# An S5 stage with its table copies moved ahead of the output writes, and merge and feed-forward blocks reordered by one tile

## What is computed

```python
_, _, s_re, s_im = lax.associative_scan(combine, (a_re, a_im, bu_re, bu_im), axis=1)
y = einsum('blgp,ghp->blgh', s_re, c_re) - einsum('blgp,ghp->blgh', s_im, c_im) + u * d_skip
y = gelu(y);  v = y @ w_glu + b_glu;  y = v[..., :D_S5] * sigmoid(v[..., D_S5:])
```

```python
x = x + g1 * ((sigmoid(pc) * y_conv + sigmoid(pa) * y_attn) @ w_out[l])
u = dwconv1d(h2 @ w_up[l], dw, dw_b);  a, g = split(u, 2)      # 3 taps, 22 tiles each
x = x + g2 * ((silu(g) * a) @ w_down[l])
```

## Time and profile before

| | |
|---|---|
| three runs | 3112.88, 3113.59, 3116.96 us (median 3113.59) |
| profiled execution | 3104.09 us, its span 3102.3 us |
| mean granted clock of TensorE | 0.968 of full speed |
| busy | PE 2876.4 us (93%), PE loads 75%, DVE 1513.3 us (49%), POOL 1266.3 us (41%), ACT 1084.9 us (35%) |
| chain that ended last | PE 77%, DVE 9%, issue 5%, DVE queue 3%, ACT 3%, DMA 1% |
| S5 stage | from about 362 us to 517.7 us of the span |
| merges of the latent passes | 1570 to 1606 us and 2611 to 2647 us |
| feed-forward blocks | 1672 to 2240 us and 2705 to 3085 us |

### The profile page before, as it was taken

One profiled execution on the slowest core, in us unless ns is written; L12 is line 12 of the kernel. 1 busy time (PEld: TensorE's weight loads), 2 busy tenths in 40 slices (PEclk: granted clock), 3 DMA queues, 4 the chain that ended last, 5 costly groups with the idle time before them and its releaser, 6 DMA issues.

```text
span 3102.3 us, 42343 instructions
## 1 busy us (share of the span) xinstructions
PE 2876.4 (93%) x15864; PEld 2340.5 (75%) x15864; DVE 1513.3 (49%) x2050; ACT 1084.9 (35%) x1593; POOL 1266.3 (41%) x696
## 2 busy tenths in 40 slices
PE   6999878999999998999889999999889998799997
PEld 6975635877777887777768888888777777687786
DVE  6865574451224453387745423313247876532324
ACT  4445122332233232236324412313243453252332
POOL 3452101443544370687523322222348773344342
PEclk9989988999999999999989999999999999899998
DMA  5227495322332333422212212212223222233231
GB/s 177 92 82 263 149 273 186 108 94 83 109 92 84 110 116 128 124 79 72 68 55 69 75 55 68 61 55 63 73 89 96 72 65 71 72 93 91 88 96 67
DMA packets 115574, 306.88 MB, mean 99 GB/s; under 512 B 36128, under 2 KB 44448, under 8 KB 114784
## 3 DMA queue, kind: packets, MB, share of 16 engines
q1 hardware_dynamic: 86000, 284.22, 29.1%
q10 hardware_dynamic: 28864, 18.76, 2.1%
q0 software_dynamic: 560, 1.84, 0.2%
HBM read 294.95 MB, written 7.45 MB: 97 GB/s over the span
## 4 chain that ended last, share of the span: by engine, by line
PE 77%; DVE 9%; issue 5%; DVEq 3%; ACT 3%; DMA 1%; ACTq 1%; POOL 0%; SPq 0%; POOLq 0%
PE ps L295 37%; PE ps L325 18%; PE ps L316 6%; PE ps L1860 3%; DVE co L2153 2%; PE ps L2266 2%; DVEq L2154 2%; PE ps L1918 2%; PE ps L1864 1%; PE ps L1865 1%; PE ps L1868 1%; DMA wraw<-stream 1%; DVE mv L2344 1%; PE ps L1937 1%; PE ps L701 1%
## 5 line engine op out<-in xcount | busy, mean ns | idle before, releaser
L256 POOL TENSOR_TENSOR wlo<-wraw,whi 128x1024 fp32r<-128x1024 f32 x373 | 923.1, 2484 | 1503.0 <-ACT whi L248 1501.6
L248 ACT ACTIVATE whi<-wraw 128x1024 fp32r<-128x1024 f32 x373 | 392.3, 1055 | 760.0 <-PE ps L316 300.8
L295 PE MATMUL ps<-xhi,whi 128*128 128x512 f32 (+1 forms) x1328 | 469.9, 370 | 1.9 <-issue 1.7
L295 PE MATMUL ps<-xlo,whi 128*128 128x512 f32 (+1 forms) x1328 | 470.6, 371 | 0.0
L295 PE MATMUL ps<-xhi,wlo 128*128 128x512 f32 (+1 forms) x1328 | 334.0, 371 | 0.0
L295 PEld LDWEIGHTS ps<-xhi,whi 128*128 128x128 f32 x1328 | 240.5, 188 | 48.7 <-issue 2.7
L295 PEld LDWEIGHTS ps<-xlo,whi 128*128 128x128 f32 x1328 | 240.5, 188 | 44.4
L295 PEld LDWEIGHTS ps<-xhi,wlo 128*128 128x128 f32 x1328 | 232.3, 188 | 44.7
L2153 DVE SCALAR_TENSOR_TENSOR co<-ub,vec,co 128x512 f32<-128x512 f32 (+1 forms) x216 | 230.1, 1105 | 5.4 <-issue 0.5
L1062 DVE SCALAR_TENSOR_TENSOR res<-ps,mod,res 128x512 f32 (+1 forms) x64 | 47.6, 748 | 266.6 <-PE ps L316 155.1
L2252 POOL TENSOR_TENSOR co<-co,ct 128x512 f32<-128x512 f32 (+1 forms) x144 | 165.2, 1147 | 20.8 <-issue 0.4
(11 more groups left out here) (396 smaller groups left out, 5614.6 us busy)
## 6 DMA issues: line engine op xcount, KB each, us to landing
wraw<-stream SPq DMA_DIRECT2D x425, 512.0 KB, 3.5
wada<-w_ada SPq DMA_DIRECT2D x56, 512.0 KB, 6.4
wraw<-w_ada SPq DMA_DIRECT2D x40, 512.0 KB, 4.0
biasb<-attn_bias ACTq DMA_DIRECT2D x32, 256.0 KB, 3.8
xin<-x0T SPq DMA_DIRECT2D x4, 528.0 KB, 6.7
s_u<-uk ACTq DMA_DIRECT2D x8, 264.0 KB, 3.3
res<-x0T ACTq DMA_DIRECT2D x1, 2048.0 KB, 8.9
s_y<-yk ACTq DMA_DIRECT2D x64, 32.0 KB, 4.1
```

Of the source, the lines that this page charges most:

```text
L248: act.activation(whi[:, s], wraw[:, s], ACT.Copy).then_inc(hi_done[s], 1)
L256: pool.tensor_tensor(wlo[:, s], wraw[:, s], whi[:, s].bitcast(F32), ALU.subtract).then_inc(lo_done[s], 1)
L295: last = pe.matmul(ps[:, bank, 0:b - a], w[:, s, kt], x[:, kt, c0 + a:c0 + b], start=start, stop=stop)
```

## The change

In the S5 stage `s5_head_act` is divided. `s5_bat_act` (the copy of `bat`) now stands between GELU and the DMAs of y; `s5_kernel_act` (`ka`, `dec`) stays behind them. Tile 0's turned tables go to PSUM banks 4 to 7, and PE does `s5_bat_pe(0)` and `s5_k_pe(0)` ahead of the last of the four single output units, `s5_w_pe(0)` right after it. DVE does `s5_diagonal(0)` and `s5_tables(1)` ahead of its last add of that projection. `ada_used` becomes one semaphore in place of eight. In the merge DVE forms `mlo` of tile m-1 after `mv` of tile m. In the feed-forward `split_hi` comes after the middle tap, and the product, the rounding and the rest of tile m-1 come after the taps of tile m (the last tile's directly behind). The `Fori` loops of both are written out. In `kv_act` the tiles rounded after the four units are (0,1), (2,3), (4), (5,6,7) in place of two each.

```diff
     def ada_worked(eng, u):
-        eng.wait_ge((lo_done if u < ADA_RAW else ada_used)[s], rnd + 1)
+        if u < ADA_RAW:
+            eng.wait_ge(lo_done[s], rnd + 1)
+        else:
+            eng.wait_ge(ada_used, u - ADA_RAW + 1)
     def s5_dve(dve):
-        s5_diagonal(dve, 0)
-        s5_tables(dve, 1)
         for i in range(NT):
     def s5_pe(pe):
         pe.wait_ge(s_m0, 1)
+        s5_w_pe(pe, 0)
+        g = U_GLU - 2
+        pe.wait_ge(acc_free[g % R], read_out(g))
+        ada_pe(pe, ADA_SSD, ADA_SSD + ADA_HEAD)
         all_freed(pe, U_GLU)
-        s5_bat_pe(pe, 0)
-        s5_k_pe(pe, 0)
-        ada_pe(pe, ADA_SSD, ADA_SSD + ADA_HEAD)
-        s5_w_pe(pe, 0)
         s5_bat_pe(pe, 1)
         s5_k_pe(pe, 1)
+    def head_bank(i):
+        return 0 if i else 4
...
             act.activation(yk[:, i % 2]..., ps[:, 6:8, ...], ACT.Gelu).then_inc(f_g.sem, 1)
+            if i + 2 < NT:
+                s5_bat_act(act, i + 2)
             act.wait_ge(f_g.sem, f_g.past("g", i))
             ...
             for k in range(LB):
                 act.dma_start(yd[i % 2]..., yk[16 * k:16 * k + 16, i % 2]).then_inc(s_yw[i % 2], 16)
             if i + 2 < NT:
-                s5_head_act(act, i + 2)
+                s5_kernel_act(act, i + 2)
...
     def raw_pe(pe, U, n, xh, xl, sums, late=None):
         for j in range(R):
+            if late and j == R - 1:
+                late()                      # s5_bat_pe(pe, 0); s5_k_pe(pe, 0)
             pe_unit(pe, U + R + j, 0, 0, xh, xl, SEQ)
...
     def kv_act(act, p, then):
-            for kt in (2 * j, 2 * j + 1):
+            for kt in ((0, 1), (2, 3), (4,), (5, 6, 7))[j]:
...
     def merge_dve(dve, p, then=None):
+        def lo(m):
+            dve.wait_ge(p.m_h.sem, p.m_h.past("hi", m))
+            dve.tensor_tensor(mlo[:, m, 0:T], mv[:, m % 2, 0:T], mhi[:, m, 0:T]..., ALU.subtract)
+        for m in range(NT):
             ... gc, ga as before ...
+            dve.tensor_tensor(mv[:, m % 2, 0:T], gc, ga, ALU.add).then_inc(p.m_v.sem, 1)
+            if m:
+                lo(m - 1)
...
     def ffn_act(act, p, q):
                     act.wait_ge(unit_done[s], rnd + 2)
-                    split_hi(act, U + 2 * j + k + R, i, 1)
                     act.wait_ge(p.f_v.sem, p.f_v.past("h", t, 2))
                     ins = act.activation(f[:, j, k, 0:T], ps[:, s, 0:T], ACT.Identity, ...)
+                    split_hi(act, g + R)
                 ... Silu of tile m ...
+                if m:
+                    hi(m - 1)
+            hi(n - 1)
...
     def ffn_dve(dve, p, q):
                 ... both units' taps of tile m ...
+                if m:
+                    gate(m - 1)             # wait silu and hi; product, rest
+            gate(n - 1)
...
             s5_tables(dve, 0)
-            for m in range(R, NT):
+            for m in range(R, NT - 1):
                 add_unit_dve(dve, U_OUT1 + m, 0, 0, m, res, SEQ, r=r)
+            dve.drain()
+            s5_diagonal(dve, 0)
+            s5_tables(dve, 1)
+            add_unit_dve(dve, U_OUT1 + NT - 1, 0, 0, NT - 1, res, SEQ, r=r)
```

More of the change, by code:

```diff
@@ L189, in build @@
     ada_landed = [sem(f"ada_landed{s}") for s in range(RA)]
-    ada_used = [sem(f"ada_used{s}") for s in range(RA)]
+    ada_used = sem("ada_used")
     s_in = [sem(f"inputs_landed{h}") for h in range(4)]
@@ L2327, in merge_dve @@
         all_freed(dve, p.U + 36)
[L2329 to L2343, removed]
-                dve.tensor_tensor(v, gc, ga, ALU.add).then_inc(p.m_v.sem, 1)
-                dve.wait_ge(p.m_h.sem, p.m_h.past("hi", m))
-                dve.tensor_tensor(mlo[:, m, 0:T], v, mhi[:, m, 0:T].bitcast(F32), ALU.subtract).then_inc(p.m_v.sem, 1)
-        if p.one:
-            body(0)
-            body(1)
-        else:
-            loop(dve, 2, body)
+        def lo(m):
+            dve.wait_ge(p.m_h.sem, p.m_h.past("hi", m))
+            dve.tensor_tensor(mlo[:, m, 0:T], mv[:, m % 2, 0:T], mhi[:, m, 0:T].bitcast(F32), ALU.subtract).then_inc(p.m_l.sem, 1)
+        for m in range(NT):
+            s, rnd = slot(p.U + 36 + m)
+            if p.one:
+                norm_add(dve, then.norm(0), m, then.T)
+            dve.wait_ge(unit_done[s], rnd + 2)
+            gc, ga = gt[:, m, 0:T], gt[:, m + NT, 0:T]
+            dve.tensor_tensor(gc, ps[:, s, 0:T], gc, ALU.mult)
+            dve.tensor_tensor(ga, ps[:, s + R, 0:T], ga, ALU.mult).then_inc(acc_free[s], 1)
+            dve.drain()
+            if p.one:
+                dve.tensor_tensor(m1[:, m, 0:T], gc, ga, ALU.add).then_inc(p.m_w.sem, 1)
+                continue
+            dve.tensor_tensor(mv[:, m % 2, 0:T], gc, ga, ALU.add).then_inc(p.m_v.sem, 1)
+            if m:
+                lo(m - 1)
+        if not p.one:
+            lo(NT - 1)
     def ffn_units(p):
@@ L2495, in ffn_dve, with gate @@
[L2495 removed]
+            def gate(m):
+                dve.wait_ge(p.f_s.sem, p.f_s.past("silu", t0 + m))
+                if m >= 2:
+                    dve.wait_ge(p.f_h.sem, p.f_h.past("hi", t0 + m - 2))
+                j = m % 2
+                dve.tensor_tensor(gated[:, j, 0:W], f[:, j, 1] if q else fs[:, j, 0, 0:T], f[:, j, 0, 0:W], ALU.mult).then_inc(p.f_v.sem, 1)
+                dve.wait_ge(p.f_h.sem, p.f_h.past("hi", t0 + m))
+                dve.tensor_tensor(hl[:, m, 0:W], gated[:, j, 0:W], h[:, m, 0:W].bitcast(F32), ALU.subtract).then_inc(p.f_v.sem, 1)
@@ new lines, in ffn_dve @@
+            for m in range(n):
+                t, j = t0 + m, m % 2
+                for k, name in enumerate("ag"):
+                    s = slot(U + 2 * m + k)[0]
+                    dve.wait_ge(p.f_a.sem, p.f_a.past(name, t))
+                    spans = [(s, 0, T)] + ([(R + s, T, W)] if q else [])
+                    for bank, a, b in spans:
+                        o = f[:, j, k, a:b]
+                        dve.scalar_tensor_tensor(o[:, 1:], ps[:, bank, 0:b - a - 1], col(f"fw0{l}", t + 22 * k), o[:, 1:], ALU.mult, ALU.add)
+                    dve.drain()
+                    for bank, a, b in spans:
+                        o = f[:, j, k, a:b]
+                        ins = dve.scalar_tensor_tensor(o[:, 0:b - a - 1], ps[:, bank, 1:b - a], col(f"fw2{l}", t + 22 * k), o[:, 0:b - a - 1], ALU.mult, ALU.add)
+                    ins.then_inc(acc_free[s], 1)
+                if m:
+                    gate(m - 1)
@@ L2654, in _ @@
             ssd_pe(pe)
-            raw_pe(pe, U_OUT1, "ssd", hhi, hlo, lambda: raw_sums_ssd(pe))
+            raw_pe(pe, U_OUT1, "ssd", hhi, hlo, lambda: raw_sums_ssd(pe), lambda: s5_first_pe(pe))
             s5_pe(pe)
```

97 lines of the change are left out of this document (43 added, 54 removed).

## The result

The changed kernel took 3090.02 us (median of 5 runs, 3080.33 to 3091.89), the kernel before 3113.59 (5 runs beside them, 3108.16 to 3117.56): ratio 0.9921, 95% interval 0.9903 to 0.9939, faster by 0.8% (the interval is 19 to 30 us). The forecast was 3101.9 with a range of 3089.0 to 3111.0: the sign and the range held, the gain was twice what I had worked out, 23.6 us for 11.7. The profiled execution went from 3104.09 to 3082.22 us, -21.9.

A forecast was written before the change was run, and what follows sets the result against it. PE, busy 93% of the span, was taken as the bound except in S5, ordered by ACT's list and y's round trip. +2.3 - 5.2 - 5.8 - 3.0 = -11.7 us gave 3092.4, plus 9.5 carried to medians: 3101.9, range 3089 to 3111.

The forecast's parts named there:

- S5: head: S5 start: turning tile 0's tables before PE's last output unit starts the chain 7.2 us earlier, less 1.4: -5.8 us.
- S5: copy ahead of the writes, tiles 0 to 4: S5 loop: y's writes wait for the `bat` copy; only 2.8 of the head's 5.8 us left, then +3.1 and +2.0.
- merges: Two merges: DVE omits its 0.79 us wait at both ends, POOL still sets 4.6 us a tile; 2.6 each, -5.2 us.
- feed-forward: Ends of six feed-forward blocks: tap ahead of `whi` shortens the chain by 0.97 us each, unrolling gives nothing; -5.8 us.
- context values: Context values: ACT's last `whi` follows an earlier rounding, on PE's path; -3.0 us.
- What is new is that y's writes wait for the copy: S5 loop on ACT: y's writes wait for the copy, the copy for PE, PE for DVE's tables two tiles ahead.
- Each such tile pays the 1.02 us of the copy: +3.1: S5 tiles 1, 2 and 3: y's round trip sets the pace, so the copy's time is added in each.
- tile 4's +2.0: S5 tile 4: writes wait 3.0 us for the turned tables, 2 counted since `ka` had to wait for PE too.
- fill the gap: Rival: earlier `wada` loads fill tile 4's idle DMA, S5 gives -12.6 instead of +2.3, 3087 us; chance 0.14.
- 6.8 us of idle DMA: S5 tile 4: idle DMA time, 15.5 x 0.44, which earlier loads could fill if DMA work sets the stage.
- slip ahead of POOL: Rival: in the merges DVE starts before POOL, giving 17.0 us instead of 5.2, 3090 us; chance 0.12.
- The burst: Rival: y's writes fall into the `wada` load burst; S5 pays +24 on top, 3126 us, slower; chance 0.07.

The follow-up runs named there:

- writes_wait: Changed kernel plus one ACT wait: the copy of `bat` must finish before y's writes are issued; 3094.5 us, ratio 0.993.
- split_first: Changed kernel with `split_hi` back ahead of the first tap in the feed-forward, the rest of the rewriting kept; 3096.24 us, ratio 0.994.
- small_loads: Changed kernel with 48 of the S5 loop's 56 `wada` loads cut to an eighth, part of the result omitted; 3075.47 us, ratio 0.989.
- lo_timed: Changed kernel, merge only: ACT splits one unit further ahead, POOL's subtraction timed to run beside DVE's gate products; 3074.82 us, ratio 0.987.
- late_and_timed: Changed kernel with the `bat` copy back behind y's writes, plus lo_timed's merge; 3074.7 us, ratio 0.988.

## Why the prediction was right in sign and short by half

| term | predicted | in the two traces | by experiment |
|---|---|---|---|
| S5: head | -5.8 | | -9.2 (164.4 to 155.3) |
| S5: copy ahead of the writes, tiles 0 to 4 | +3.0 + 3.1 + 2.0 | writes held 4.5 us longer | +3.6 (155.3 to 158.9) |
| S5 in all | +2.3 | -5.1 | -5.6 |
| merges | -5.2 | -2.63 and -2.65 | |
| feed-forward | -5.8 | 3 x 1.30 + 3 x 1.28 = -7.7 | 6 x 1.03 + 6 x 0.27 |
| context values | -3.0 | -3.0 | |
| sum | -11.7 | -21.1, and -0.8 between | |

The sign of the whole held by the last three terms, which came out near their sizes or above. S5 was forecast slower and became faster, and the missing gain is mostly there.

**The step that failed: "What is new is that y's writes wait for the copy", and with it "Each such tile pays the 1.02 us of the copy: +3.1" and tile 4's +2.0.** They are held only where the copy itself waits for PE: in tile 0 in every trace of the early order (1.8 us longer in the changed kernel, up to 2.9 in others, for my 3.0), and in tile 2 in two of the three traces with the changed kernel's S5 code (2.7 and 2.9 us). In the changed kernel tiles 1, 3, 4 and 5 issue their first write 0.6 us after GELU, as before. So the 8.1 us that I charged were 3.6. writes_wait made the step true and brought 6.0 us, which is most of the 7.4 by which the stage was off.

**The head was mis-sized too,** -9.2 for -5.8. At GELU of tile 0 it gives 6.1 us (35.9, 36.1 and 36.6 us into the stage with the old head, 29.9 to 30.3 in all kernels with the new), close to the 5.8. Another 3 us come in the loop behind it, and only with the late copy (124.4 and 126.0 us from GELU of tile 0 to the GLU quad, for 128.7 and 127.6). By the table above they do not lie in the landings, which sum to 37.8 and 40.4 us for 39.4 and 39.1, but mostly between read and rounding, 36.7 and 37.6 for 39.4 and 39.7. What shortens that way was not tried and stays open.

**The merges** came out at 2.6 each for the reason given, the 0.79 us at both ends, with POOL's turn setting 4.6 us between. Wrong was that `mv` would still take 1.8 and PE's last wait fall to 1 or 2: the waits that went are short ones ahead of it, in layer 0's merge before these two:

```profile
1578.44 0.47 PE L295 MATMUL ps<-hhi,whi 128*128 128x512 f32 x1 [1.00 <-DVE gt L2338]
...
1596.63 0.47 PE L325 MATMUL ps<-mhi,whi 128*128 128x512 f32 x1 [1.35 <-DVE gt L2338]
```

**The feed-forward** is 1.03 for 0.97, and 0.27 a block that I had put at nothing with "no row shows on PE's path". split_first shows that the rest of the rewriting is on that path; whether the loop's own instructions or the order of the waits bring it was not divided.

**The rivals.** The loads did not fill the gap (S5 -12.6), but they were the larger cost, and my bound for them, 6.8 us of idle DMA, was the wrong way to price it: small_loads gives 14. DVE did not slip ahead of POOL. The burst did not come: one tile of the changed kernel landed in 12.4 us, but its six landings sum to 39.1 us, for 39.4 before.

**By size.** 7.4 us of the missing 10.2 (21.9 - 11.7) are S5's, 1.9 the feed-forward's, 0.1 the merges', and 0.8 lies between. On top, the medians gained 1.7 us more than the profiled executions: the 9.5 us that I carried over were 7.8. The 0.8 is the rest of larger shifts that cancel, for which the prediction has no term. First the stretch behind layer 0's merge and layer 0's feed-forward in the kernel before, then in the changed kernel (length, then PE's busy time; at the end clock, DMA share, GB/s):

```profile
1605.80:1672.24 66.44, 61.49 (x286) 52.28 (x286) 29.11 (x47) 22.80 (x37) 20.12 (x8) 0.90 0.21 64
1672.24:2246.34 574.10, 554.63 (x3096) 484.44 (x3096) 184.80 (x291) 177.25 (x224) 163.06 (x68) 0.98 0.20 63
```

```profile
1596.68:1659.79 63.11, 58.22 (x286) 48.76 (x286) 29.69 (x48) 22.80 (x37) 20.12 (x8) 0.96 0.23 70
1659.79:2226.28 566.49, 550.92 (x3096) 481.28 (x3097) 201.60 (x291) 168.43 (x217) 163.22 (x68) 0.99 0.20 63
```

The same matmuls take 3.3 and 3.7 us less at a higher mean granted clock. Ahead of layer 1's merge it is the other way: from the last context wait to that merge 325.7 us at 0.98 before, 330.1 at 0.97 after. Whether the shorter waits raise the clock is not shown, but split_first, whose three waits there are 3.1 us longer, takes 572.9 us for layer 0's feed-forward, where the twelve traces with the changed kernel's feed-forward code take 565.1 to 569.3.

## What to carry to other kernels

Before you charge an instruction to the DMAs that follow it in an engine's list, ask what they wait for: here the queue issued them while the engine still worked, but a wait for another engine that stood ahead of them in the list held them too. Where a small round trip through memory stands in the chain, price it by its landing beside the large loads (1.7 us alone, 3.6 to 12.4 beside them in the changed kernel), and by the sum over all tiles, since which tile gets the long landing changes between traces of one code. And where two engines exclude each other, start the slower one beside the instructions that are let through; that was worth 9.6 us in two short stages, for 5.3 by the order of the code around them. A gain in one stage can be lost in the next: in lo_timed and late_and_timed the stretch behind layer 0's merge took 66.6 us at a granted clock of 0.90, for 63.1 at 0.96.

## What the runs showed of the hardware that was not expected

ACT's queue issued y's writes 0.14 us after a 1.02 us copy had begun that stood ahead of them.

DVE's `mv` ended 0.55 us after POOL's `wlo` in three traces, wherever it began: 1.1 us behind POOL's start before (1.82 us long), 0.2 us behind it after (2.75), 1.2 us in lo_timed (1.74). POOL's instruction takes 2.35 to 2.40 us in all three.

The first 350 us, same code in all kernels, differ by up to 14.6 us between traces. In the window from 300 to 340 us PE's mean granted clock was 0.91 in the changed kernel, which reached the ruler's mark at 353.3, and 0.74 in lo_timed, which reached it at 365.5. So lo_timed's profiled execution looks only 1.7 us shorter than the changed kernel's while its merges are 9.6 us shorter. A total can't be read without its stages.
